# Gate products of 256 columns in a decoder trunk: ScalarE copies the high halves, VectorE adds the low halves

## The reference, cut to what matters

```python
e = take(i1, ci // 16) * 128 + take(i2, ci % 16)      # 8 heads x 16 picks = 128 experts for each token
g = softmax(sc).reshape(tokens, 128)
a = gelu(einsum('td,ted->te', hb, u[e]))
out = einsum('te,ted->td', g * a, v[e])
```

## Time and profile before

| | us |
|---|---|
| median of 3 runs | 2211.7 (2194.89 to 2211.74) |
| the profiled execution | 2211.71 |
| its span | 2209.8 |
| TensorE busy | 2155.0 |
| VectorE busy | 1125.3 |
| ScalarE busy | 608.4 |

### The profile page before, as it was taken

How to read it: one execution, slowest core, us unless ns; L and a number is a source line. 1 busy time by engine, 2 the same in 40 slices (tenths; PEclk the granted TensorE clock), 3 DMA queues, 4 the chain that set the end, 5 groups by cost and what they waited for, 6 DMA issues and landing times.

```text
span 2209.8 us, 30856 instructions
## 1 busy us (share of the span) xinstructions
PE 2155.0 (98%) x12924; PEld 1464.6 (66%) x12924; DVE 1125.3 (51%) x2470; ACT 608.4 (28%) x1026; POOL 180.9 (8%) x272
## 2 busy tenths in 40 slices
PE   6999999989899999999999999999999999999999
PEld 4733435668688888898898988888444444444444
DVE  4197636452687993555554442230554554554452
ACT  0102122210123233333333333232233233233231
POOL 0001000000054650000000000000400000000000
PEclk9999969559999999999999999999999999999999
DMA  3232512001121343444444444542967667556551
GB/s 139 79 84 95 185 43 91 1 3 58 39 77 44 130 173 116 173 173 192 191 192 192 191 173 188 187 162 108 323 192 241 207 199 236 200 183 227 199 182 39
DMA packets 131690, 326.21 MB, mean 148 GB/s; under 512 B 22888, under 2 KB 88664, under 8 KB 115168
## 3 DMA queue, kind: packets, MB, share of 16 engines
q1 hardware_dynamic: 128080, 316.34, 40.1%
q0 software_dynamic: 3472, 7.91, 1.5%
HBM read 250.95 MB, written 73.27 MB: 147 GB/s over the span
## 4 chain that ended last, share of the span: by engine, by line
PE 96%; DVE 3%; DMA 1%; ACT 0%; issue 0%; SPq 0%; DVEq 0%; ACTq 0%
PE psum L1696 31%; PE psum L1741 29%; PE psum L1465 27%; PE psum L1717 5%; PE psum L1534 1%; PE psum L1471 1%; DMA g_in<-d_gate 0%; DVE sdm L1089 0%; DMA xT<-in_xT 0%; DVE v_lo L1388 0%; DVE rstd L846 0%; DVE mtmp L845 0%; DVE mtmp L844 0%; DVE hraw L1118 0%; DVE w_f L1397 0%
## 5 line engine op out<-in xcount | busy, mean ns | idle before, releaser
L1696 PE MATMUL psum<-h_hi,u_hi 128*128 128x260 bf16 x2048 | 395.1, 274 | 0.7 <-ACT Ssb L752 0.7
L1696 PE MATMUL psum<-h_lo,u_hi 128*128 128x260 bf16 x2048 | 393.7, 273 | 0.0
L1696 PE MATMUL psum<-h_hi,u_lo 128*128 128x260 bf16 x2048 | 393.5, 273 | 0.0
L1741 PE MATMUL psum<-w_hi,v_hi 128*128 128x512 bf16 x1024 | 388.1, 379 | 1.2 <-DVE w_lo L1404 1.2
L1741 PE MATMUL psum<-w_hi,v_lo 128*128 128x512 bf16 x1024 | 388.1, 379 | 0.0
L1741 PE MATMUL psum<-w_lo,v_hi 128*128 128x512 bf16 x1024 | 388.1, 379 | 0.0
L1255 DVE TENSOR_TENSOR u_lo<-u_raw,u_hi 128x1024 bf16<-128x1024 f32 x128 | 152.5, 1218 | 367.0 <-ACT u_hi L760 367.0
L1397 DVE TENSOR_TENSOR w_f<-a_in,g_in 128x512 f32<-128x512 f32 x128 | 87.9, 686 | 297.6 <-PE psum L1741 245.9
L1696 PEld LDWEIGHTS psum<-h_hi,u_hi 128*128 128x128 bf16 x2048 | 200.4, 98 | 29.7 <-issue 0.8
L1696 PEld LDWEIGHTS psum<-h_lo,u_hi 128*128 128x128 bf16 x2048 | 198.1, 97 | 31.0
L1696 PEld LDWEIGHTS psum<-h_hi,u_lo 128*128 128x128 bf16 x2048 | 198.2, 97 | 30.8
(11 more groups left out here) (311 smaller groups left out, 2175.8 us busy)
## 6 DMA issues: line engine op xcount, KB each, us to landing
u_raw<-in_uT SPq DMA_DIRECT2D x32, 2048.0 KB, 10.3
v_raw<-in_v SPq DMA_DIRECT2D x32, 2048.0 KB
d_act<-act_f SPq DMA_DIRECT2D x32, 1024.0 KB, 4.8
d_gate<-stage SPq DMA_DIRECT2D x16, 2048.0 KB, 6.3
a_in<-d_act SPq DMA_DIRECT2D x32, 1024.0 KB
g_in<-d_gate SPq DMA_DIRECT2D x32, 1024.0 KB
wr<-in_w SPq DMA_DIRECT2D x13, 2048.0 KB, 7.7
kv<-in_ck SPq DMA_DIRECT2D x24, 256.0 KB, 4.3
```

The source lines that it names most:

```text
L1696: mm = pe.matmul(upair[n % 2][:, f, 0:HALF], w[g % 2][:, k, c * P:(c + 1) * P], hs[:, k, halves[f]], start=(k == 0 and x == 0), stop=(k == ...
L1741: mm = pe.matmul(ybank[m], w[g % 2][:, c, m * P:(m + 1) * P], z[g % 2][:, c, :], start=(g == 0 and c == 0 and x == 0), stop=(g == NG - 1 a ...
```

## The change

The high and the low product of a token become one product of 256 columns, whose two halves land side by side in PSUM and are no longer added there. A quad now fills two banks, and only two quads fit in the four banks, so `gates(q)` waits for quad q - 2 in place of q - 4. ScalarE copies the high halves of a quad into `stage` and signals `gl_high`. VectorE then adds the low halves out of PSUM onto `stage` (`add_gate_parts`, 128 passes of 512 values) and signals `gl_ev`, which still frees the bank and the store. VectorE does the two adds of a pair two steps after it built this pair's operands (`GATE_LAG = 2`), behind `u_low` and `gate_rows` of that step. `AT_V` goes from 96 to 98.

```diff
-AT_V = 96
+AT_V = 98
+GATE_LAG = 2
+    def gate_parts(q):
+        pair = pa[:, 4 + 2 * (q % 2):6 + 2 * (q % 2), :]
+        return pair.rearrange("p j (t x e) -> p x e (j t)", t=2, x=2)
@@ ScalarE, evacuate(q)
-                A(stage[n % 2][:, :, at:at + 4], gbank[q % 4].rearrange("p (t e) -> p e t", t=4), ACT.Copy
-                  ).then_inc(gl_ev, 1)
+                A(stage[n % 2][:, :, at:at + 4], gate_parts(q)[:, 0, :, :], ACT.Copy).then_inc(gl_high, 1)
@@ VectorE
+            def add_gate_parts(q):
+                n = q // QUADS
+                v.wait_ge(gl_high, q + 1)
+                at = 4 * (q % QUADS)
+                part = stage[n % 2][:, :, at:at + 4]
+                tt(part, part, gate_parts(q)[:, 1, :, :], ALU.add).then_inc(gl_ev, 1)
@@ VectorE, loop over n
                 if 0 <= n - AT_GATES < NPAIRS:
                     gate_rows(n - AT_GATES)
+                if 0 <= n - AT_GATES - GATE_LAG < NPAIRS:
+                    add_gate_parts(2 * (n - AT_GATES - GATE_LAG))
+                    add_gate_parts(2 * (n - AT_GATES - GATE_LAG) + 1)
@@ TensorE, gates(q)
-                if q >= 4:
-                    pe.wait_ge(gl_ev, q - 3)
+                if q >= 2:
+                    pe.wait_ge(gl_ev, q - 1)
                 for t in range(4):
-                    for part in range(2):
-                        mm = pe.matmul(gbank[q % 4][:, t * P:(t + 1) * P], oneR[u % PRING][:, q % 2, :, t],
-                                       gateL[u % PRING][:, part, q % 2, :, t], start=(part == 0), stop=(part == 1))
+                    at = (t % 2) * 2 * P
+                    mm = pe.matmul(gbank[2 * (q % 2) + t // 2][:, at:at + 2 * P], oneR[u % PRING][:, q % 2, :, t],
+                                   gateL[u % PRING][:, :, q % 2, :, t], start=True, stop=True)
                 mm.then_inc(gl_mm, 1)
```

More of the change, by code:

```diff
@@ L344, in trunk_and_peer @@
     qz_zero, s_used, rank_steps, one_hot, looked = sems("qz_zero scores_used rank_steps one_hot_ranks looked_up")
-    keys_set, tb_made, tb_read, gl_one, gl_L, gl_R, gl_mm, gl_ev = sems(
-        "keys_set tb_made tb_read gl_one gl_L gl_R gl_mm gl_ev")
+    keys_set, tb_made, tb_read, gl_one, gl_L, gl_R, gl_mm, gl_high, gl_ev = sems(
+        "keys_set tb_made tb_read gl_one gl_L gl_R gl_mm gl_high gl_ev")
     g_stored, a_stored, as_stored = ([sem(f"{n}{b}") for b in range(2)] for n in ("g_stored", "a_stored", "as_stored"))
```

## The result

| | before | after |
|---|---|---|
| median, us | 2211.7 (4 runs) | 2325.8 (4 runs, 2323.57 to 2326.58) |
| span of the profiled execution, us | 2209.8 | 2324.0 |
| ratio of times | | 1.0534, 95% interval 1.0484 to 1.0584 |

What follows compares the result with a forecast made beforehand. TensorE, without a gap while gates are made, was taken as the bound. 2211.7 - 7 (products) + 92 + 2.5 (waits) + 30 (clock) = 2329, say 2330 us, slower by 5.3%; own range 2300 to 2365, wider range 2275 to 2365.

Steps and rivals of the forecast that it cites:

- The bound: While gates are made, TensorE alone bounds without a gap: 5.37 us up products, 1.90 us gate products, 64 times.
- The new wait: Gates wait for adds behind `u_low`, which waits for ScalarE's rounding: 15 x 6.16 us, and 2.5 us once at n = 28.
- The products: 1024 gate products of 128 columns become 512 of 256, spaced 223 ns: 7 us gained, bounds 0 and 61.
- the split of the 118 ns: Spacing of a 128-column gate product: 109 ns of streaming plus about 10 ns once for each product.
- The row of 278 ns: Profile row: a run's first gate product, weights already loaded, lasts 278 ns; read as the operand streaming at half rate.
- The Trainium skill's rule: Two values per 16-byte line read at full bandwidth; then the weight load sets the spacing, gain 61 us; that rival 15%.
- The clock: TensorE's idling at stalls halves its clock, slowing work afterwards: 15 x 2.0 = 30 us, bounds 0 and 65.
- the dense row: Profile row: after 9.01 us idle with dense work behind, the clock was back 4.7 us after restart, costing 2.4 us.
- The work of the adds, two quads, transfers: VectorE's step grows from 3.55 to 4.75 us, under TensorE's 7.15; adds, copies and transfers are hidden, costing nothing.
- a cover of some 5 us: On SyncE, three transfers one after another take 21.4 us; weights arrive 29 us into a group of 34.8, so hidden.

Runs made afterwards that it cites:

- run 1: Changed kernel with VectorE's two adds of a step moved ahead of `u_low`: 2191.9 us, ratio 0.9971 to the kernel before.
- run 2: Changed kernel with the adds between `u_low` and `gate_rows`: 2281.6 us, ratio 1.0370 to the kernel before.
- run 11: Changed kernel with `GATE_LAG` 1 instead of 2, nothing else: 2192.3 us, ratio 0.9994 to the kernel before.
- run 5: Kernel before with only the streamed operand `gateL` packed, one token's 128 columns as neighbours: 2476.8 us, ratio 1.1233.
- run 3: Changed kernel with 48 further TensorE products filling the wait at every fourth step: 2295.5 us, ratio 1.0412 to the kernel before.
- run 4: Kernel before with two PSUM banks rotating for the gates instead of four: 2206.4 us, ratio 1.000.
- run 6: Kernel before with only the weights `oneR` packed, `gateL` keeping its step: 2254.4 us, ratio 1.0255.
- run 7: Changed kernel with the adds ahead of `u_low` and `gateL` packed, products of 256 columns: 2546.5 us, ratio 1.1584 to the kernel before.
- run 8: Kernel before with both `gateL` and `oneR` packed, products of 128 columns: 2722.0 us, ratio 1.2356.
- run 10: Changed kernel with adds ahead of `u_low`, `oneL` and `gateL` packed, VectorE passes without a step: 2158.4 us, ratio 0.9824 to the kernel before.
- run 9: Kernel before with `oneL` and `gateL` packed and VectorE's passes without a step, products of 128 columns: 2152.9 us, ratio 0.9763.

## Why the prediction was right, point by point

- **The bound.** TensorE's chain without a gap, so any wait counts in full: right, the account closes within 0.2 us.
- **The new wait.** Place, number and length were right. Forecast 15 x 6.16 and 2.5 once, 94.9 us; measured 92.2 idle and 2.6 of lost overlap, 94.8. Shown by runs 1, 2 and 11: the adds moved ahead of `u_low` or one step earlier take all of it away, moved halfway they take away what the passes between cost. What made the number sharp was to follow four engines' orders for one step and to add the durations from one place of the trace; busy shares (VectorE is busy half the time) would have said the adds are free.
- **The products.** The mechanism was right: streaming with a step, not the load. The size was a little off. Forecast 223 ns for 256 columns and 7 us gained; measured 1.84 / 8 = 230 ns and 3.5 us. The step that was mis-sized is the split of the 118 ns: (230 - 118) / 128 = 0.875 ns a column and 6 a product, where 0.81 and 10 were taken. The row of 278 ns pointed the right way, and its reading is confirmed by run 5. The Trainium skill's rule (SBUF — State Buffer, cachelines), by which two values in a line of 16 bytes give full bandwidth, doesn't hold for this operand: 0.875 ns a column with two bfloat16 values in each 16 bytes, and (219 - 169) / 127 = 0.39 once packed. The same note says that each crossing to a new line costs something, without a size; whether the loss here is of that kind, no run shows.
- **The clock.** Right that it falls; its price was too high. Forecast 15 x 2.0 = 30, measured 23.1 over 16 stalls, 1.4 each. The term halved the 4.7 us of the dense row (2.4) and took 2.0, because some stalls might bring no fall; in fact all did, and so did the short one at n = 28. What was wrong is the halving of the whole low time. Of the 5.1 us at one place the first 2.0 are gate products, which take 2.00 us at either clock (run 3); only the up products behind them slow down, (5.1 - 2.0) / 2 = 1.55, and their piece there is 6.92 - 5.37 = 1.55 us longer.
- **The work of the adds, two quads, transfers.** Hidden, as forecast: runs 1 and 4 show the first two. The weights were never late for `u_high` in the changed kernel's trace. The forecast added three transfers one after another and found a cover of some 5 us; they overlapped. At the place shown, the load of the weights was issued from 959.6 to 961.3, no such load took over 14.2 us to land, and the next `u_high` began at 987.8: a cover of at least 12 us.

The forecast of 2330 against 2325.8 is partly a balance: the clock was 7 us too high, the products' gain 3.5 too high.

## What to carry to other kernels

Before work that an engine must wait for is put into another engine's order, look for the waits that this order already has. A wait that costs nothing today is charged in full to whoever comes to stand behind it, while the busy share of the engine says nothing of it; the remedy is the order, or one step of lag, not less work. And when a product of few columns costs more than its columns, check the step of its streamed operand before its width: here the layout was worth 64 us with the right order, the width 3.6 at best.

## What the runs showed of the hardware that was not expected

- Streaming bfloat16 with a step of 8 bytes costs 0.875 ns a column at full clock and no more at half: from a standing start eight products of 256 columns took 2.00 us at 0.50 (changed kernel) and 2.00 at 1.00 (run 3). Packed, the same side follows the clock: 1.87 and 1.05 us for 16 products.
- A VectorE pass of 1024 bfloat16 values takes 0.68 us as the kernel had it (innermost four neighbours), 1.22 us with a value repeated along the innermost axis, and 4.70 to 4.95 us in the mean if it writes with a step of 256 bytes (runs 5 to 8).
- An idle time of 3.6 us brought the clock down 15 times out of 15, and cost as much afterwards (22.8 us) as idle times of 6 us (23.1 us over 16 stalls). In run 2 each fall came only after TensorE had started again. Idle times of 1.4 us (run 10) and 0.69 us (run 9) brought none.
